# Stick-breaking stage of a two-layer hybrid encoder: its steps ordered by a written plan of six parts per head pair

## The reference, cut to what matters

```python
def stick_breaking_attention(q, k, v):
    ...
    def block(q_start, nq):
        nk = q_start + nq
        z = jnp.einsum('bqhd,bkhd->bhqk', qf[:, q_start:nk], kf[:, :nk])
        ...
        causal = s[None, :] < t[:, None]
        log_beta = jax.nn.log_sigmoid(z)
        log_1m = jnp.where(causal, log_beta - z, 0.0)
        tail = lax.cumsum(log_1m, axis=3, reverse=True) - log_1m
        a = jnp.where(causal, jnp.exp(log_beta + tail), 0.0)
        return jnp.einsum('bhqk,bkhd->bqhd', a, vf[:, :nk])
    outs = [block(0, N_META)]
    outs += [block(N_META + i * SB_BLOCK, SB_BLOCK) for i in range(S // SB_BLOCK)]

def hybrid_layer(h, pos, norm_g, w_in, w_out, sinks):
    u = rmsnorm(h, norm_g)
    proj = jnp.einsum('bld,de->ble', u, w_in)
    ...
    sb_o = stick_breaking_attention(...) * jax.nn.silu(sb_g)
    sw_o = sliding_window_gqa(rope(sw_q), rope(sw_k), sw_v, sinks) * jax.nn.silu(sw_g)
    return h + jnp.einsum('bld,de->ble', jnp.concatenate([sb_o, sw_o], -1), w_out)
```

## Time and profile before

| | |
|---|---|
| median of three runs | 1200.52 us |
| the profiled execution | 1198.98 us |
| its span | 1197.2 us |
| PE busy | 1159.2 us (97%) |
| DVE busy | 713.0 us (60%) |
| ACT busy | 455.9 us (38%) |
| stick stage of layer 0, from the first scores to the first window scores | 72.89 to 391.24 |
| the same of layer 1 | 653.34 to 970.48 |

### The profile page before, as it was taken

The page is one execution under the profiler, slowest core; times in us unless marked ns, Lnnn a source line. Parts: engine busy times, 40 slices in busy tenths (PEclk is TensorE's granted clock), DMA queues, the critical chain, the costliest instruction groups (busy, mean ns, idle before and its releaser), DMA issues.

```text
span 1197.2 us, 22343 instructions
## 1 busy us (share of the span) xinstructions
PE 1159.2 (97%) x8682; PEld 1085.5 (91%) x8682; DVE 713.0 (60%) x1418; ACT 455.9 (38%) x1237; POOL 2.6 (0%) x5
## 2 busy tenths in 40 slices
PE   7999999999999999999999999999999999999998
PEld 6989998989989989899999899899899998888998
DVE  6656565556367577754584564655544856866533
ACT  7324333344344345521232432443334434453113
POOL 0000000000000000000000000000000000000000
PEclk9999999999999999999999999999999999999999
DMA  5621020111131121141322111102121312205203
GB/s 199 244 54 50 24 60 26 50 36 44 39 69 48 23 58 51 42 173 36 143 73 74 45 41 41 50 24 58 28 50 44 73 32 50 58 2 177 67 7 141
DMA packets 123576, 77.83 MB, mean 65 GB/s; under 512 B 42304, under 2 KB 116032, under 8 KB 123472
## 3 DMA queue, kind: packets, MB, share of 16 engines
q1 hardware_dynamic: 122608, 75.08, 21.7%
q10 hardware_dynamic: 864, 1.32, 0.4%
HBM read 49.82 MB, written 12.71 MB: 52 GB/s over the span
## 4 chain that ended last, share of the span: by engine, by line
PE 87%; DVE 6%; ACT 3%; issue 3%; DMA 1%; SPq 0%; DVEq 0%; ACTq 0%
PE psum L903 40%; PE psum L891 20%; PE psum L984 6%; PE psum L967 5%; PE psum L955 4%; PE psum L958 3%; PE psum L1016 2%; PE psum L1081 1%; PE psum L1053 1%; DVE mix L1426 1%; PE psum L1028 1%; PE psum L1046 1%; DVE WL L1479 1%; DVE UL L1436 1%; ACT P_late L1313 1%
## 5 line engine op out<-in xcount | busy, mean ns | idle before, releaser
L903 PE MATMUL psum<-UH,WH 128*128 128x384 f32 (+2 forms) x1632 | 534.2, 327 | 7.5 <-DVE UL L1436 4.6
L903 PE MATMUL psum<-UL,WH 128*128 128x384 f32 (+2 forms) x1632 | 522.7, 320 | 0.0
L891 PE MATMUL psum<-UH,WL 128*128 128x384 f32 (+2 forms) x1632 | 517.0, 319 | 1.3 <-DVE WL L1479 1.3
L903 PEld LDWEIGHTS psum<-UH,WH 128*128 128x128 f32 x1632 | 307.0, 188 | 13.0 <-DVE UL L1436 5.2
L891 PEld LDWEIGHTS psum<-UH,WL 128*128 128x128 f32 x1632 | 307.0, 188 | 1.9 <-DVE WL L1479 1.9
L903 PEld LDWEIGHTS psum<-UL,WH 128*128 128x128 f32 x1632 | 307.6, 188 | 0.1
L1299 ACT ACTIVATE PT<-psum 128x512 f32<-128x512 f32 (+5 forms) x260 | 116.8, 492 | 19.7 <-PE psum L967 18.3
L1290 ACT ACTIVATE X<-psum 128x264 f32<-128x264 f32 (+9 forms) x240 | 91.5, 435 | 49.5 <-PE psum L958 48.6
L1560 DVE TENSOR_TENSOR_SCAN X<-X,stick 16x16 f32<-16x16 f32 (+5 forms) x144 | 99.2, 730 | 13.4 <-ACT X L1290 12.6
L967 PE MATMUL psum<-ident,X 128*128 128x128 f32 x576 | 85.9, 274 | 6.0 <-ACT Vn L1253 4.9
L1563 DVE TENSOR_TENSOR_SCAN X<-X 128x352 f32<-128x352 f32 (+4 forms) x96 | 86.2, 937 | 3.7 <-ACT X L1290 3.7
(11 more groups left out here) (181 smaller groups left out, 1178.8 us busy)
## 6 DMA issues: line engine op xcount, KB each, us to landing
w_raw<-in_w_in SPq DMA_DIRECT2D x36, 512.0 KB, 4.3
h_spill<-X SPq DMA_DIRECT2D x16, 520.0 KB, 6.7
X<-h_spill SPq DMA_DIRECT2D x16, 520.0 KB, 5.4
w_raw<-in_w_in SPq DMA_DIRECT2D x32, 256.0 KB, 3.7
q_swap<-qk_even SPq DMA_DIRECT2D x64, 64.0 KB, 2.9
q_swap<-qk_odd SPq DMA_DIRECT2D x64, 64.0 KB, 2.6
w_raw<-in_w_out SPq DMA_DIRECT2D x16, 256.0 KB, 3.0
w_raw<-in_w_out SPq DMA_DIRECT2D x32, 128.0 KB, 3.3
```

Of the source, the lines that this page charges most:

```text
L891: return pe.matmul(out_columns, WL[:, j % 2, k, :], UH[:, k, uses], start=False, stop=(k == KT - 1))
L903: pe.matmul(out_columns, WH[:, j % 2, k, :], u[:, k, uses], start=(k == 0 and u is UH), stop=False)
```

## The change

`lagged`, `merge`, `WEIGHT`, `waiting` and `flush` go. A table `STICK_PLAN` takes their place: six parts per head pair. In a part, `"T50"` means R (if the tile group is the block's first), then the transpositions of both heads for block 5, group 0; `"Z60"` the scores of block 6, segment 0; `"fill"` the next projection task; `"next0"` and `"next1"` the first two scores of the next pair. The `AV` and `AV_rest` of all tile groups of a part follow at its end, in one run. In the first pair the first two scores, which `next0` and `next1` cover for the others, come right after the first chunk of k, with `AV_rest` of block 0 after its third. PE's wait for q and k now names the chunk that the block ends in, where it was all three at block 0.

```diff
-WEIGHT = dict(Z=1.0, q_swap=0.0, T=0.6, R=0.0, AV=0.6, AV_rest=0.15)
+STICK_PLAN = [["T10", "Z20", "fill", "Z30", "T20", "Z40", "fill"], ["T30", "Z41", "fill", "Z50", "T40", "Z51", "fill"],
+              ["T50", "Z60", "fill", "T51", "Z61", "fill"], ["T60", "Z70", "fill", "T61", "Z71", "fill"],
+              ["T70", "Z80", "fill", "Z81", "T71", "Z82", "fill"], ["T80", "fill", "next0", "T81", "next1", "fill"]]
...
             q[0] += [("q_swap", 0, b) for b in range(Q_RING)]
+            k[0] += stick_scores(0, 0, 0) + stick_scores(0, 1, 0) + [("R", 0, 0)]
+            k[2].append(("AV_rest", 0, 0))
...
+    def sb_attention(p, fill):
+
+        out = []
+        for part in STICK_PLAN:
             values = []
...
+            for word in part:
+                if word == "fill":
+                    out += fill.pop(0)
+                elif word[0] == "Z":
+                    out += stick_scores(p, int(word[1]), int(word[2]))
+                elif word[0] == "T":
+                    b, n = int(word[1]), int(word[2])
+                    tiles = tuple(range(4 * n, min(4 * n + 4, b)))
+                    out += [("R", p, b)] * (n == 0) + [("T", p, b, h, tiles) for h in range(2)]
+                    values += [("AV", p, b, tiles, n == 0)] + [("AV_rest", p, b)] * (4 * n + 4 >= b)
+                elif p + 1 < PAIRS:
+                    b = int(word[4:])
+                    out += stick_scores(p + 1, b, 0) + [("R", p + 1, 0)] * b
+                    values += [("AV_rest", p + 1, 0)] * b
+            out += values
+        return out
...
-        steps += merge(sb_attention(p), fill, 0.5)
-    flush = lagged([], [])
+        steps += sb_attention(p, fill)
...
-                    if b == 0:
-                        pe.wait_ge(q_in.sem, q_in.at(l, 3 * p + 3))
-                        pe.wait_ge(k_in.sem, k_in.at(l, 3 * p + 3))
+                    if i == 0:
+                        ready = 3 * p + chunk_of(q_start(b) + n_queries(b) - 1) + 1
+                        pe.wait_ge(q_in.sem, q_in.at(l, ready))
+                        pe.wait_ge(k_in.sem, k_in.at(l, ready))
```

More of the change, by code:

```diff
@@ L186, in swa_fill @@
         return delayed(tasks)
[L188 to L201, removed]
-            values = []
-            if b == 0:
[L204 to L219, removed]
@@ new lines, in stick_scores @@
+    def stick_scores(p, b, i):
+        step, later = ("Z", p, b, i), divmod(p * BLOCKS + b + Q_RING, BLOCKS)
+        return [step] + [("q_swap",) + later] * (i + 1 == len(key_segments(b)) and later[0] < PAIRS)
+    def sb_attention(p, fill):
+        out = []
+        for part in STICK_PLAN:
+            values = []
+            for word in part:
[14 more added lines that the diff above has]
+        return out
@@ L252, in swa_attention @@
         return out + [("gate", 2), ("split", 2, 3), ("split_low", 2, 3)]
[L254 to L267, removed]
     flat = lambda tasks: [step for task in tasks for step in task]
@@ L272, in layer_steps @@
         fill = sb_unit(p + 1) if p + 1 < PAIRS else window[:12]
-        steps += merge(sb_attention(p), fill, 0.5)
-    flush = lagged([], [])
+        steps += sb_attention(p, fill)
     tail = window[12:30]
     tail[-1] = tail[-1] + flat(window[30:])
-    steps += flush + swa_attention(tail + [[("proj", IN_TILES + i, c)] for i, c in EARLY_OUTS])
+    steps += swa_attention(tail + [[("proj", IN_TILES + i, c)] for i, c in EARLY_OUTS])
     first_outs = [(0, 0), (1, 0), (0, 1), (1, 1), (0, 2), (1, 2)]
```

## The result

The changed kernel takes **1186.17 us** in the median of four runs (1185.38 to 1186.79), the kernel before beside it 1200.56 (1198.09 to 1201.11): a ratio of 0.988, 95% interval 0.987 to 0.990. The forecast was 1186.5 in a range of 1180.5 to 1193.0. The profiled execution took 1186.79 us with a span of 1185.0, against 1198.98 and 1197.2: 12.2 us less in the span.

A forecast was written before the change was run, and what follows sets the result against it. PE's queue was taken to bound the stick stage, busy 311.81 of 318.35 us. Terms summing to -13.3 gave 1185.7 from the profiled 1198.98, or 1187.2 by the median; forecast 1186.5, range 1180.5 to 1193.

The forecast's parts named there:

- Terms 1 and 2: Stick stage: 56 fewer runs of values save 20.1 us; new neighbours of transpositions, projections and scores cost 1.3.
- Term 3: Scores that wait for ACT to read their bank: -2.3 us, between -6.6 and +2.
- Term 4: Transpositions behind `turn_v` wait for ACT's copies six times instead of four, +3.1 us; at `turn_sv` in the last pair +1.2.
- Term 5: First pair, queries: block 2's `q_swap` is issued before k's second projection, so its wait goes: -2.4 us.
- Term 6: First pair, k: first scores follow the first chunk, a longer path through ACT and DVE: +1.0 us.
- Term 7: Last pair: block 6's transpositions wait for scans behind `rope_add` on DVE: +4.0 us, bounds nil to +7.
- Term 8: Stage end: first window scores wait longer for `rope_low`, as DVE sets this end: +0.9 us.
- slower: Rival: the price of value runs shows up at other joints when runs are merged; 1204.5 us, chance 0.03.
- Longer waits: Rival: transpositions opening each part wait for late DVE scans, +8 us, 1194.5; chance 0.13.
- Waits that go: Rival: terms 4 and 7 at their lower bounds, +1.5 us rather than +8.3, 1179.7; chance 0.09.
- three signs of error: Value runs still costing 0.35 each beyond their work, scan waits in pairs 0 to 2, last pair's wait over 3 us.

The follow-up runs named there:

- e1: Changed kernel with each part's first group of value steps ahead of its last projection, 49 runs of values per layer instead of 25: 1208.22 us.
- e9: The edit of e1 put into the changed kernel with the moves of e3, e5, e6 and e7 together (1163.73 us): 1184.56 us.
- e7: Changed kernel with block 5's short transpositions ahead of the query projection, no longer right behind `turn_v` or `turn_sv`: 1181.45 us.
- e5: Changed kernel with the first pair's split of weight tile 5 moved behind the `q_swap` of block 4: 1182.22 us.
- e3: Changed kernel with the first pair's first two scores after k's second projection instead of its first: 1179.47 us.
- e6: Changed kernel with the last pair's first `rope_add` behind the scores of block 6 on DVE's queue: 1181.93 us.
- a0: The changed kernel run once more without any edit, as reference for the other runs: 1187.97 us.
- b0: The kernel before the change, run once more for its first pair: 1199.56 us.

## Why the prediction was right, point by point

Sign and size were right, 0.3 us from the median, and the main mechanism, fewer runs of values, was right too. But that the sum came so near, -13.3 for the measured -12.2, is in part luck: errors of both signs, up to 4 us each, cancelled in it.

- **Terms 1 and 2, runs of values and new neighbours: right, if anything too small.** -18.8 were worked out. e1 and e9 give 0.33 to 0.35 and 0.34 for a run and what follows it, where the forecast had 0.31 and 0.35 by kind of follower. The "issue" waits fell further than said (to 7.4 us, not 9).
- **Term 3, scores that wait for their bank: right.** By start-to-start distances 6.6 us became 4.4: -2.2 for -2.3.
- **Term 4, transpositions behind transposed values: right.** Six waits as said. The values' transpositions and the wait behind them take 1.94 us start to start in all six places; before, they took 1.94 in four and 0.64 in pair 0's two, and the short transpositions that follow now take some 0.06 more than without a wait: 2 x 1.30 + 6 x 0.06, +3.0 for +3.1. At `turn_sv` the second head's transposition is 0.63 later in each layer: +1.3 for +1.2. e7 showed that these are waits for a bank and go when scores take that place.
- **Term 5, `q_swap`: wrong.** "Now it is issued before k's second projection" holds for block 2, and its wait is gone. But the swap of block 4 took over the place behind the weight load, and the scores of block 4 lose 1.65 and 1.80: +1.0 in all for -2.4. The step that failed is the sentence on DMAs, "each `q_swap` at least one" projection ahead of use, and with it the sign "the `q_swap` wait is gone"; it counted the distance from the step in the list and not from when SP is free to issue it. e5 showed the cause.
- **Term 6, the first scores: the mechanism right, the size wrong.** The wait is 2.38 for 1.84, +1.1 for +1.0. Not seen was what a longer pause does to the clock: 4.3 more in this profile (k's second chunk takes 6.55 and 5.79 for the 4.28 that e5 shows at full clock, the second scores of layer 0 0.90 for 0.48). The forecast had no term for it. e3 took both away.
- **Term 7, the last pair's rope: right place, too large.** Four waits on L1547 as said, but +2.4 start to start for +4.0. The DMAs landed earlier: DVE begins at 344.56, 3.5 behind the first transposition that follows `turn_sv` (341.10), and not 4.5 as in the earlier trace rows. e6 showed that it is the rope on DVE.
- **Term 8, the stage's end: right.** 0.67 idle for 0.24, 0.93 for 0.49 start to start: +0.9 in both layers.
- **Not in the sum.** The measured terms give -18.8 - 2.2 + 3.0 + 1.3 + 1.0 + 1.1 + 4.3 + 2.4 + 0.9 = -7.0, where the first number is the forecast's own, and the span says -12.2. Of the missing 5.2, 2.1 are the first scores of the next pair: 0.55 before and 0.11 now, and 0.10 of the difference is in term 1, so 0.35 less in 6 places. The second scores came right behind them and waited for their bank; now eight transpositions lie between. Term 3 counted no such case. PE's timeline of the kernel before (first line) and after:

```profile
151.92 0.34 PE L955 MATMUL psum<-qk_odd 128*128 128x144 f32 x1 [0.29 <-ACT X L1290]
...
148.69 1.09 PE L951 MATMUL psum<-ident,X 128*128 128x128 f32 x8
149.54 0.31 PE L939 MATMUL psum<-qk_odd 128*128 128x144 f32 x1
```

Some 2 more are the 56 runs, if each is worth 0.035 more than the forecast had, as e1 and e9 have it. About 1 stays unassigned.

Of the rivals, "slower" rested on a run costing under 0.1: e1 and e9 rule it out. (Its 1204.5 counts from the profiled execution, and the forecast from 0.8 above that; it makes no difference.) "Longer waits" did not come in pairs 0 to 2. "Waits that go" did not come either: the waits of term 4 are all there. Two of the three signs of error that the text named did not occur: no wait on scans in pairs 0 to 2, and the last pair's wait is under 3 us. The third, value runs that "still cost 0.35 each more than their work", can't tell right from wrong, since the forecast itself puts a run at 0.31 with what follows it.

## What to carry to other kernels

Count what a change of matmul shape costs by start-to-start distances at the joints, in a row of each kind, and then multiply by how often the order of steps makes it: here it was worth more than any wait. When steps are moved, follow each queue (SP's above all) as a queue: an issue that moves out from behind a blocked one leaves the next in its place. And look at the granted clock behind the longer pauses (1.4 us and more here), since a pause can cost twice its own length, and does so in some executions only.

## What the runs showed of the hardware that was not expected

- **The clock falls behind some pauses and not behind others of the same length.** Of 12 pauses of 2.38 us (a stage's first scores, in the first profile of the changed kernel and in a0, e1, e5, e6, e7), 10 were followed by a granted clock of 0.50 for some 3 to 7 us, at a cost of 1.5 us each (the shorter falls) or 2.7 to 2.9 (the longer): from the first scores to the first value step 9.8 or 11.0 to 11.2 us pass, and 8.2 to 8.3 where the clock stays full (e5, e6). Of the 4 pauses of 1.84 none was; of 2 of 1.88 (e7), one; behind the `q_swap` wait of block 4 (1.25 to 1.68 us, 12 places in the profiles of the changed kernel, a0, e1, e3, e6 and e7), two, one in a0 (1.63) and one in e1 (1.68). Other waits of that length were followed by one too: the wait of 1.4 for DVE in the second window stage in 2 of 12 profiles (b0 and e1), and the wait of 1.54 at a stage's end in 1 of 4 places (e1); behind the wait of 1.68 for DVE at some 34 us, in all 12 profiles, there was none. No length was found that decides alone, and what does decide is open. The fall can be dearer than the pause.
- **A run of 64-column value matmuls among full-width ones costs 0.33 to 0.35 us** (e1 and e9): 0.08 ahead of it, 0.16 at its ends, 0.11 in the projection behind it.
